# One layer of a conformer, latent-attention and conv-FFN decoder: both ends of the up stage ordered anew, the residual stored in thirds, the rings of the down stage laid out anew

## The reference, cut to what matters

```
z  = x @ w_in + b_in                      # conformer branch, latent attention, gates
mix = (g_conv * y_conv + g_mla * y_mla) @ w_mix_out
x1 = layer_norm(ALPHA * x + mix) * ln1_g + ln1_b
h  = causal_depthwise_conv(ffn_state, x1 @ w_up, width 3) + bias     # 2 * D_FF channels
hg, hv = split(h)
y  = layer_norm(ALPHA * x1 + (silu(hg) * hv) @ w_down)
```

## Time and profile before

| what | us |
|---|---|
| median of 3 runs (2042.5 to 2046.49) | 2042.72 |
| the profiled execution, its own time | 2043.98 |
| its span, first to last instruction | 2042.1 |
| PE busy (share of the span) | 1968.6 (96%) |
| PE weight loads busy | 1811.1 (89%) |
| DVE busy | 1303.9 (64%) |
| POOL busy | 915.3 (45%) |
| ACT busy | 842.5 (41%) |
| mean granted TensorE clock, of full speed | 0.987 |

### The profile page before, as it was taken

How to read it: one execution, slowest core, us unless ns; L and a number is a source line. 1 busy time by engine, 2 the same in 40 slices (tenths; PEclk the granted TensorE clock), 3 DMA queues, 4 the chain that set the end, 5 groups by cost and what they waited for, 6 DMA issues and landing times.

```text
span 2042.1 us, 34425 instructions
## 1 busy us (share of the span) xinstructions
PE 1968.6 (96%) x13460; PEld 1811.1 (89%) x13460; DVE 1303.9 (64%) x1712; ACT 842.5 (41%) x1443; POOL 915.3 (45%) x511
## 2 busy tenths in 40 slices
PE   8999999999999999989999999779999999899998
PEld 8999999999988999866669998779999999767886
DVE  3999999946755665645443327577777777645352
ACT  4222222226237677653441114345354444444342
POOL 4712444412111010134312256488878788576574
PEclk9999999999999999999999999889999999999999
DMA  6422223215420000156534431232222222676463
GB/s 218 152 91 69 94 93 110 81 62 191 138 75 23 16 13 16 63 211 267 230 141 158 123 105 53 106 94 64 90 69 85 74 84 74 193 245 207 149 222 115
DMA packets 189550, 238.12 MB, mean 117 GB/s; under 512 B 20558, under 2 KB 149088, under 8 KB 185294
## 3 DMA queue, kind: packets, MB, share of 16 engines
q1 hardware_dynamic: 169536, 159.09, 24.9%
q0 software_dynamic: 8320, 46.27, 5.9%
q10 hardware_dynamic: 11549, 30.69, 4.0%
HBM read 188.71 MB, written 48.15 MB: 116 GB/s over the span
## 4 chain that ended last, share of the span: by engine, by line
PE 83%; DVE 7%; ACT 3%; issue 3%; DMA 2%; SPq 1%; POOL 1%; ACTq 0%; DVEq 0%
PE ps L2480 32%; PE ps L3135 14%; PE ps L2673 9%; PE ps L3202 8%; PE pst L3135 5%; PE pst L3202 3%; PE ps L2887 2%; PE pst L2752 1%; PE ps L2940 1%; PE pst L2919 1%; DMA inr<-f_d 1%; DMA xr_d<-res 1%; PE ps L2741 1%; PE ps L2739 1%; PE pst L2922 1%
## 5 line engine op out<-in xcount | busy, mean ns | idle before, releaser
L1552 POOL TENSOR_TENSOR wlo<-wraw,whi 128x1024 fp32r<-128x1024 f32 x66 | 160.0, 2429 | 387.0 <-ACT whi L860 292.1
L1822 DVE SCALAR_TENSOR_TENSOR pst<-g_ext,wtap,pst 128x512 f32<-128x512 f32 x464 | 306.9, 748 | 0.0
L2480 PE MATMUL ps<-xh,whi 128*128 128x352 f32 x864 | 187.2, 325 | 1.2 <-ACT stat L954 1.2
L2480 PE MATMUL ps<-xh,wlo 128*128 128x352 f32 x864 | 186.2, 323 | 0.0
L2480 PE MATMUL ps<-xl,whi 128*128 128x352 f32 x864 | 186.0, 323 | 0.0
L2373 DVE TENSOR_TENSOR x1l<-inr,x1h 128x384 fp32r<-128x384 f32 (+1 forms) x66 | 87.7, 1348 | 105.3 <-ACT x1h L1444 105.2
L2480 PEld LDWEIGHTS ps<-xh,whi 128*128 128x128 f32 x864 | 147.0, 189 | 1.9 <-issue 1.8
L2480 PEld LDWEIGHTS ps<-xh,wlo 128*128 128x128 f32 x864 | 148.4, 188 | 0.0
L2480 PEld LDWEIGHTS ps<-xl,whi 128*128 128x128 f32 x864 | 146.7, 188 | 0.0
L1755 POOL TENSOR_TENSOR wlo<-pieces,whi 128x1024 fp32r<-128x1024 f32 x44 | 110.7, 2523 | 72.5 <-ACT whi L1438 72.5
L1628 POOL TENSOR_TENSOR wlo<-wraw,whi 128x1024 fp32r<-128x1024 f32 (+1 forms) x12 | 24.2, 2032 | 245.9 <-ACT whi L1038 245.9
(11 more groups left out here) (501 smaller groups left out, 5601.0 us busy)
## 6 DMA issues: line engine op xcount, KB each, us to landing
pieces<-in_w_down SPq DMA_DIRECT2D x44, 512.0 KB, 4.8
wraw<-in_w_in SPq DMA_DIRECT2D x37, 512.0 KB, 3.9
f_d<-hv SPq DMA_DIRECT2D x22, 528.0 KB, 2.7
wraw<-in_w_down SPq DMA_DIRECT2D x22, 512.0 KB, 4.2
wraw<-in_w_up SPq DMA_DIRECT2D x40, 256.0 KB, 3.8
x1f<-in_w_up SPq DMA_DIRECT2D x40, 256.0 KB, 4.0
inr<-f_d SPq DMA_DIRECT2D x44, 192.0 KB, 2.5
xt_d<-tmp POOLq DMA_DIRECT2D x8, 528.0 KB, 3.5
```

Of the source, the lines that this page charges most:

```text
L1552: nc.gpsimd.tensor_tensor(wlo[:, n % HL, :], wraw[:, n % RAW, :], whi[:, n % HL, :].bitcast(F32), ALU.subtract).then_inc(lo_done, 1)
L1822: half[x] = link(nc.vector.scalar_tensor_tensor(out=dst, in0=src, scalar=tap(k_), in1=pst[:, x, :], op0=ALU.mult, op1=ALU.add))
L2480: last = nc.tensor.matmul(out[:, c, 0:CH], w[:, k, :], x[:, k, c * CH:(c + 1) * CH], start=(k == 0 and x is hi_x and w is wh), stop=(k == ...
```

## The change

1. `res` gets the rest of its bias by thirds (`rest(c)`, ACT), and SP stores it by thirds (`residual_out(c)`), each as soon as it is whole; the first behind the layer norm's first third.
2. The four token combinations get a region of their own: all `t_sum` go to `tf`, `t_low` to the same bytes, `t_high` over `res`. So `token_sum` no longer waits for the store, and `token_high` does.
3. `first_tap` is taken out of `whole_product`, and the order on ACT, DVE and POOL at the start of the up stage is new. `token_low` is now on DVE for n = 0, 2, 3 and on POOL for n = 1 alone; products 3, 4, 6 of pair 0 wait for DVE's, product 2 for POOL's.
4. The rings of the down stage lie elsewhere (`F0 = HF`: inner rows in the right halves of the columns; raw weights in the left halves), so that within pair 19 SP can issue three `inner_load`, four `down_load` and the residual, ahead of `inner_out(20)`.
5. PE counts each step of round 0 alone, ahead of the sample step, and a raw slot is freed by `raw_read`: an even step x only behind step x + 2, an odd one behind step x + 1.
6. The last sample step stands between the tails of tiles 0 and 1; `y_scale`, `normalise` and the copy of the sample parts move by one or two steps.

The diff, cut to its core:

```diff
+        F0 = HF
-        t_sum = (res[:, lowk, left], tf[:, 0, :, :], res[:, lowk, right], res[:, highk, left])
-        t_high = (tfr[:, 2, :, :], tfr[:, 1, :, :], tfr[:, 3, :, :], resr[:, highk, right])
-        t_low = (resr[:, lowk, left], tfr[:, 0, :, :], resr[:, lowk, right], resr[:, highk, left])
+        t_sum = tuple(tf[:, n, :, :] for n in range(4))
+        t_low = tuple(tfr[:, n, :, :] for n in range(4))
+        t_high = (resr[:, lowk, left], resr[:, highk, right], resr[:, lowk, right], resr[:, highk, left])
+        def raw_read(x):
+            return (x | 1) + 2 if x < FT else x + 1
...
# SP
+            def residual_out(c):
+                sp.wait_ge(l1_s, AS[f"z{c}6"])
+                sp.wait_ge(l1_g, GS[f"l{c}7"])
+                sp.dma_start(xr_d[:, :, part3(c)].rearrange("k p n -> p k n"), res[:, :, part3(c)]).then_inc(xr_out, 16)
...
 (down_load)
                 elif d < RD:
-                    sp.wait_ge(w_used, UP_P0 + 7 * (NP - 1) + 6)
+                    sp.wait_ge(w_used, UP_P0 + 7 * (NP - 1) + 2)
                 else:
-                    wait_used(sp, d - RD + 1)
+                    wait_used(sp, raw_read(d - RD))
 (inner_load)
-                if x < FR:
-                    sp.wait_ge(w_used, UP_P0 + 7 * (NP - 1) + x // HK + 1)
-                else:
-                    wait_used(sp, x - FR + 1)
+                if x == HK - 1:
+                    sp.wait_ge(mg_done, UP_V0 + 7 * NP)
+                elif HK <= x < FR:
+                    sp.wait_ge(w_used, UP_P0 + 7 * (NP - 1) + 6)
+                elif x >= FR:
+                    wait_used(sp, raw_read(x - FR))
 (residual_load)
-                    sp.wait_ge(w_used, UP_P0 + 7 * (NP - 1) + (5 if r else 3))
+                    sp.wait_ge(w_used, UP_P0 + 7 * (NP - 1) + (7 if r else 4))
...
+            for c in range(3):
+                residual_out(c)
             up_load(0)
...
+                if i == NP - 1:
+                    for x in range(3):
+                        inner_load(x)
+                    for d in range(2, RD):
+                        down_load(d)
+                    residual_load(0)
                 inner_out(i + 1)
# ACT
             def token_high(n):
                 for x in range(2):
-                    act.wait_ge(l1_v, T_ADD0 + 2 * T_TURN.index(n) + x + 1)
+                    act.wait_ge(xr_out, 48)
+                    act.wait_ge(l1_v, T_ADD0 + (x + 1, 6, 6, 8)[n])
...
             full(1, 5, 7)
+            rest(0)
             high(2, *range(MT))
             full(2, 5, 7)
             hi(up_block(1, 1))
-            for k in (0, 2, 4, 6):
...
-            for cols in (left, right):
-                act.dma_start(xr_d[:, :, cols].rearrange("k p n -> p k n"), res[:, :, cols]).then_inc(xr_out, 16)
+            rest(1)
+            rest(2)
...
# DVE
             def token_sum(n):
-                if n != 1:
-                    dve.wait_ge(xr_out, 32)
+                if n == 0:
+                    dve.wait_ge(l1_s, AS["z26"])
+                    dve.wait_ge(l1_g, GS["l27"])
...
                 if i == NP - 1:
-                    for x in range(4):
+                    for x in range(3):
                         inner_low(x)
+                    residual_scale(0)
                 gate_right(i)
                 value_left(i)
-            residual_scale(0)
...
# PE
                         last = down_step(r, t, k)
+                    last.then_inc(w_used, 1)
                     if r == 0 and k % 2:
-                        last = sample_step(k - 1)
-                    if r == 1 or r == 2 or k % 2:
-                        last.then_inc(w_used, 1 if r else 2)
+                        sample_step(k - 1)
```

More of the change, by code:

```diff
@@ L312, in down_raw @@
             x = d % RD
-            return two(wraw[:, x, :]) if x < 2 else pieces[:, :, x + 2, 3 * P:3 * P + 512]
+            return two(wraw[:, x, :]) if x < 2 else pieces[:, :, x + 2, 0:512]
         rr = [at(f"rr{j}", [P, MT, 3 * P], F32, X0 + 3 * XB + j * 2 * QB) for j in range(2)]
@@ L1353, in full, with rest @@
                     step(f"x{c}{k}", biased(c, k, res))
+            def rest(c):
+                for k in (0, 2, 4, 6):
+                    act.wait_ge(l1_v, VS[f"l{c}{k}"])
+                    step(f"z{c}{k}", biased(c, k, res))
             hi(N4 + 2)
@@ L1477, in _ @@
             hi(up_block(1, 1))
[L1478 to L1485 removed]
+            rest(1)
+            rest(2)
             whole_product(0, 0)
+            first_tap(0, 0)
             whole_product(0, 1)
+            first_tap(0, 1)
+            token_high(0)
             up_high(0, 0)
@@ L1506, in _ @@
                 first_part(i)
+                if i == 0:
+                    for e in (4, 5, 6):
+                        up_high(0, e)
+                if i == NP - 1:
+                    for x in range(3):
+                        inner_high(x)
                 if more:
@@ L1517, in _ @@
                     down_high(1)
-                    for x in range(FR):
-                        if x == 4:
-                            down_high(2)
-                        inner_high(x)
+                    down_high(2)
+                    down_high(3)
+                    inner_high(3)
                 first_tap(i + 2, 0)
@@ L1525, in _ @@
                     up_high(i + 1, 6)
+            for x in range(4, FR):
+                inner_high(x)
             for j in range(4):
                 act.sem_inc(y_out[j], 16)
-            down_high(3)
             for d in range(HL, 3 * FT):
                 down_high(d)
+                if d == FT + 1:
+                    act.wait_ge(ql_t, SP_T0 + 1)
+                    nc.scalar.activation(sparts[:, :], p_parts[:, 0, :], ACT.Copy).then_inc(ql_r, 1)
+                for i in {24: (0,), 25: (1,), 29: (2,), 45: (3,), 47: (4,), 49: (5,)}.get(d, ()):
+                    y_scale(i)
                 if d + HL < 3 * FT:
@@ L1536, in _ @@
                     state_rows_out()
-                if d == 23:
-                    act.wait_ge(ql_t, SP_T0 + 1)
-                    nc.scalar.activation(sparts[:, :], p_parts[:, 0, :], ACT.Copy).then_inc(ql_r, 1)
-                for i in {25: (0,), 26: (1,), 29: (2,), 45: (3,), 47: (4,), 49: (5,)}.get(d, ()):
-                    y_scale(i)
             for i in (6, 7, 8):
@@ L1732, in up_weights @@
                 up_low(i, 5)
-                if i == 0:
-                    token_low(3)
                 up_low(i, 6)
@@ L2387, in _ @@
             token_sum(0)
+            conv(0, 0)
             token_sum(1)
-            conv(0, 0)
+            token_sum(2)
             token_sum(3)
-            token_sum(2)
-            token_low(0)
             conv(0, 1)
             inner(0)
-            token_low(2)
+            for n in (0, 2, 3):
+                token_low(n)
             for i in range(NP):
@@ L2445, in _ @@
             conv(FT - 1, 0)
+            for x in range(HK, FR):
+                inner_low(x)
+            conv(FT - 1, 1)
             inner_low(FR)
-            conv(FT - 1, 1)
             inner_low(FR + 1)
```

74 lines of the change are left out of this document (33 added, 41 removed).

## The result

| what | before | after |
|---|---|---|
| median of the runs, us | 2042.84 (2042.5 to 2046.49) | 2023.18 (2021.57 to 2027.13) |
| ratio, 95% interval | 1 | 0.9903 [0.9884, 0.9921] |
| the profiled execution, its own time | 2043.98 | 2023.47 |
| its span | 2042.1 | 2021.6 |
| DVE busy | 1303.9 | 1304.2 |

The kernel became 19.7 us faster; 30.4 had been forecast, and the time lies just above the upper end of the range (2023.0). The spans differ by 20.5 us, and they divide so: pair 1 starts at 1336.19 instead of 1357.97, minus 21.8 (forecast minus 29.3); pairs 1 to 19 minus 0.7; from the end of pair 19 to round 1 plus 0.2 (forecast minus 1); the rest plus 1.8 (forecast 0).

The account below looks back on a forecast made before the run. PE was taken to bound pairs 1 to 19 (busy 392.53 of 392.6 us), with losses in pair 0 and round 0; 2043.98 - 29.3 - 1.1 = 2013.6, median 1.26 lower, 2012.3 us; range 2003 to 2023.

Parts of the forecast that it names:

- The store by thirds: Start of up stage: residual stored in thirds of 3.9 us, done about 1289.5, weights about 1293 instead of 1299.46.
- six low parts at the slower price: DVE in pair 0: low parts beside POOL at 6.89 us for two, ready about 1306.5, 1310 and 1313.
- POOL is what is late next: Pair 0: POOL's chain ends at 1312.4, PE wants product 2 at 1313.9; it fits by 1.5 us.
- Rival B: Pair 0: POOL, standing still for DVE's two-input work, is late for product 2 by 4.3 us; 2018.1 us; chance 0.15.
- The hand-over: Pair 19 to down stage: residual lands 3 or 4 us before the pair ends; PE's 6.5 us wait goes.
- plus what is queued ahead: Hand-over: unpriced addition to the residual load's 5.26 us for loads ahead of it in the queue.
- Round 0: Down stage: later refills cost 9.2 us of waits and 4.5 of half clock; 90.7 against 91.8 us, minus 1.
- Rival A: Round 0: refills do not bind, so it takes 83 us, 7.7 less than forecast; 2004.6 us; chance 0.18.
- C: Rival: PE waits in every pair of round 0 and the clock stays at half; 155 us, total 2076.6; chance 0.04.
- The rest: Rounds 1 and 2 and the tail of the down stage: unchanged.

Follow-up runs that it names:

- no_low3: Changed kernel with DVE's low part of combination 3 left out, product 6 of pair 0 taking combination 2's instead; one run, 2022.8 us.
- pool_waits: Changed kernel with POOL beginning pair 1's weights only behind DVE's add for product 2 of pair 0; 2028.71 us, ratio 0.9932.
- end_only: Changed kernel with the start of the up stage undone, keeping the new hand-over and down stage; 2049.6 us, ratio 1.0040 to before.
- free_early: Changed kernel with round 0's raw slots freed by the sample steps' own count instead of the step behind them; 2012.85 us, ratio 0.9851.
- start_only: Changed kernel with the hand-over and down stage undone, keeping the new start of the up stage; 2018.05 us, ratio 0.9883 to before.
- small_two: Changed kernel with the residual loaded behind two weight loads instead of four, and sample sums copied ahead of inner tile 26's high part; 2018.69 us, 0.9883.
- low_merged: Changed kernel with each of DVE's three low parts made in one instruction of both halves instead of two; ratio 0.9910.
- combo_merged: Changed kernel with the edits of free_early and small_two, plus DVE's low parts merged into three instructions; 2009.19 us, ratio 0.9837.

## Why the prediction was right and wrong

**The store by thirds: right.** The three DMAs are issued from 1270.23 on, and the last has landed by 1290.60, where ACT's `token_high(0)` starts after waiting for it (forecast 1289.5); POOL has the weights at 1293.69 (forecast 1293). `whole_product` no longer stands behind the store, and pair 0 starts at 1306.03, where 1308.0 and, if the clock stays up, 1306.5 were forecast.

**The failed step: DVE, "six low parts at the slower price".** It read 6.89 us as the price of two combinations and got 10.2 us for three (1303 to 1313). The row is for two instructions, which make one combination, so by its own price three cost 20.7; they took 16.05. The step also ended there: behind the low parts `conv(1, 0)` (7.0 us) and `gate_left(0)` stand in the same list, and product 5 needs the latter. With 10.2 us `gate_left` would have come at 1321 (an estimate: 1326.67 less the 5.85 us), in time for product 5 at 1322.1; with 16.05 it came at 1326.67. But the price is the smaller part of the error: in no_low3 the low parts took 11.53 us, and PE still waited 4.56 us at pair 1, for `value_right(0)` at the end of the list. Of the lost time at pair 1 only 2.6 us went with those 4.5. By this run the larger part of the failed step is that it stopped counting DVE's list at the low parts, with both halves of `conv(1)`, `inner(1)` and five additions behind them, the last of which empties the bank that pair 1 needs. From pair 0 to pair 1 it took 30.2 us instead of 20.66: 7.2 of waits and 2.3 of half clock behind them. That is more than the forecast missed by (7.5 us at pair 1), since pair 0 began 2 us earlier than said. "POOL is what is late next" was wrong: PE waited 0.68 us for POOL in pair 0. (The 20.66 us are themselves a mean that holds pair 1's 21.9; the pairs behind it took 20.59 before.)

**Rival B: the mechanism was right, its place wrong.** DVE and POOL do stop each other for whole instructions, as the rows of 0.53 and 2.55 us and the run pool_waits show. But B let POOL stand still for all of DVE's work; in fact they alternate, one instruction each, and it was DVE's list that PE had to wait for.

The Trainium skill (SBUF — State Buffer, Who interferes with whom) states the exclusion for two SBUF inputs, names `tensor_scalar` among what can also contend, and excepts instructions with one SBUF input otherwise; the trace agrees in all three: additions of one PSUM and one SBUF operand take 0.7 us beside POOL or not, and the scaling 1.36 or 3.49.

**The hand-over: half right.** The wait was said to go, since the residual would land 3 or 4 us early. It was issued at 1719.33 behind four weight loads of 512 KB and landed at 1727.7, after 8 us instead of 5.26; "plus what is queued ahead" was named and not priced. 2.0 us of wait and 1.6 of half clock stayed; 0.9 of the wait is a turn with POOL, since the scaling took 2.27 us instead of 1.36. And that DVE would scale it in time was assumed; end_only shows that it need not.

**Round 0: right in kind, in size partly by luck.** Step 9 waited 4.48 us (forecast 3.1), two others 0.20 and 0.69 (1), the tail 2.68 (5.1): 8.05 against 9.2, a wait 1.4 us too short and one 2.4 too long that nearly cancel. The whole from pair 19's end on came to 91.9 instead of 90.7. But the forecast took the later refill for something that the hand-over pays back; free_early shows that it alone takes 8 us of round 0 (start_only, with the old rule, has the same 82 us), which is what made the end a loss. Rival A (refills don't bind) is out, C too: 0.94 of full clock in the round.

**The rest: forecast 0, measured plus 1.8.** 1.50 us of it is the wait for `sparts`, ACT's copy of the sample sums. The copy stands behind the high part of inner block 26, and SP could load that block only when the tail had read its slot. SP and ACT in after, then SP in before:

```profile
1819.52 0.33 SPq L794 DMA_DIRECT2D inr<-f_d  x1
1821.94 0.53 ACT L1470 ACTIVATE x1h<-inr 128x384 fp32r<-128x384 f32 x1 [8.70 <-DMA inr<-f_d]
```
```profile
1829.92 0.33 SPq L782 DMA_DIRECT2D inr<-f_d  x1
```

After the change the load is issued 0.5 us ahead of round 1; before the change it was issued 12.4 us ahead. So this is the later refill once more, which the forecast followed only within round 0: it goes when slots are freed earlier (free_early, D minus 1.7) as well as when the copy stands ahead of that block (small_two).

## What to carry to other kernels

Price a list of VectorE instructions beside a busy POOL by turns: each waits for up to one whole POOL instruction, so small ones suffer most, and count the list up to the instruction that frees PE's next bank, not up to the one in question. A slot of a ring should be freed by its own last reader; one coarser step cost 8 us in 92, and 1.7 behind them. A lag that engines off the path take along from the start comes due where the loop ends, even if none of them is busy all the time: look at what each waits for, not only at its busy share.

## What was not expected of the hardware

- The size of the turns: 0.26 us becomes 1.27, 1.29 becomes 2.30 or 3.4 by the length of the other engine's instruction.
- DVE is busy for 74% of pairs 1 to 19, and yet in seven of the fourteen kernels the lag lasted through all of them, since DVE waited for ACT in every pair. In the other seven it ended within one to three pairs, once it began to fall: in after DVE's first tap came 2.82 us behind the pair's start in pair 8, and 1.88, 0.96 and 0.82 us in pairs 9, 10 and 11. low_merged and combo_merged, alike in pair 1 (5.55 and 5.57 us), stood at 0.87 and 3.99 us in pair 3. In start_only it stayed at 2.82 to the end. What lets it fall or stay was not settled.
- combo_merged's five runs lie between 2008.04 and 2016.47 us; only the slowest has a trace, so whether the others differ by a late DVE at the hand-over is not shown.
